# The input projection's feature blocks as seven block products instead of eight, in a hybrid mLSTM/HGRN2/attention inference step

## What is computed

```python
sh1, sc1, g1, sh2, sc2, g2 = jnp.split(ada, 6, axis=-1)
h = _rmsnorm(x, p['norm1_g']) * (1 + sc1) + sh1
proj = h @ p['w_in']
(mq, mk, mv, mo, mg, hq, hf, hi, hg, aq, ak, av, bg) = _split(proj, IN_SIZES)
```

## Time and profile before

| | |
|---|---|
| median of 3 runs | 2395.26 us (2395.05 to 2397.84) |
| the profiled execution's own time | 2394.08 us |
| its span, first to last instruction | 2392.3 us |
| mean granted PE clock | 0.993 |
| PE busy | 2318.2 us, 97% |
| DVE, ACT, POOL busy | 1274.8, 789.2, 225.4 us |

### The profile page before, as it was taken

How to read it: one execution, slowest core, us unless ns; L and a number is a source line. 1 busy time by engine, 2 the same in 40 slices (tenths; PEclk the granted TensorE clock), 3 DMA queues, 4 the chain that set the end, 5 groups by cost and what they waited for, 6 DMA issues and landing times. The chain is left out here.

```text
span 2392.3 us, 43619 instructions
## 1 busy us (share of the span) xinstructions
PE 2318.2 (97%) x17767; PEld 2142.3 (90%) x17767; DVE 1274.8 (53%) x2027; ACT 789.2 (33%) x1329; POOL 225.4 (9%) x244
## 2 busy tenths in 40 slices
PE   6999999999999899999999999998999999999997
PEld 5887779999999899889899999877999999998886
DVE  4331110102445376675455546778676676667877
ACT  5321111113333233323444445325232232234444
POOL 0000000000110011111121101000121121120001
PEclk9999999999999999999999999999999999999999
DMA  6324532215442523314100218421222122159434
GB/s 277 119 84 185 185 139 85 103 68 192 163 156 99 190 87 101 99 65 155 47 18 18 88 65 330 159 94 60 84 101 103 68 102 102 70 172 276 128 102 124
DMA packets 124748, 290.64 MB, mean 121 GB/s; under 512 B 19744, under 2 KB 63216, under 8 KB 115264
## 3 DMA queue, kind: packets, MB, share of 16 engines
q1 hardware_dynamic: 88944, 222.15, 27.3%
q10 hardware_dynamic: 31696, 51.26, 5.8%
q0 software_dynamic: 3968, 15.21, 1.7%
HBM read 205.47 MB, written 83.17 MB: 121 GB/s over the span
## 5 line engine op out<-in xcount | busy, mean ns | idle before, releaser
L62 PE MATMUL ps<-h_hi,fill_whi 128*128 128x384 f32 x672 | 234.9, 350 | 4.0 <-PEq L82 3.4
L62 PE MATMUL ps<-h_lo,fill_whi 128*128 128x384 f32 x672 | 225.8, 336 | 3.7 <-issue 3.7
L62 PE MATMUL ps<-wt 128*128 128x320 f32 (+2 forms) x1046 | 227.2, 327 | 2.3 <-DVE merged L2927 1.3
L62 PE MATMUL ps<-h_hi,fill_wlo 128*128 128x384 f32 x672 | 225.9, 336 | 0.0
L62 PE MATMUL ps<-ys,mergedr 128*128 128x256 f32 (+1 forms) x1056 | 219.2, 296 | 0.4 <-issue 0.4
L62 PE MATMUL ps<-zb,mergedr 128*128 128x320 f32 (+2 forms) x764 | 200.3, 327 | 4.9 <-issue 2.7
L62 PE MATMUL ps<-zb,wt 128*128 128x384 f32 (+3 forms) x758 | 200.2, 325 | 0.0
L62 PEld LDWEIGHTS ps<-wt 128*128 128x128 f32 x1046 | 179.6, 189 | 16.6 <-issue 2.6
L62 PEld LDWEIGHTS ps<-ys,mergedr 128*128 128x128 f32 x1056 | 174.2, 190 | 0.7 <-issue 0.7
L62 PE MATMUL ps<-prj_whi,h_hi 128*128 128x512 f32 (+1 forms) x432 | 165.4, 383 | 4.5 <-DVE h_lo L626 4.5
L62 PE MATMUL ps<-prj_wlo,h_hi 128*128 128x512 f32 (+1 forms) x432 | 162.5, 376 | 0.0
(11 more groups left out here) (459 smaller groups left out, 4800.0 us busy)
## 6 DMA issues: line engine op xcount, KB each, us to landing
wraw<-in_w_ffn_in SPq DMA_DIRECT2D x22, 1024.0 KB, 5.0
prj_raw<-in_w_ada SPq DMA_DIRECT2D x16, 1024.0 KB, 6.0
fill_raw<-in_w_fill SPq DMA_DIRECT2D x30, 512.0 KB, 4.0
wtf<-a_dram SPq DMA_DIRECT2D x55, 256.0 KB, 2.6
bg_dram<-fill_st ACTq DMA_DIRECT2D x72, 192.0 KB, 2.0
xf<-bg_dram POOLq DMA_DIRECT2D x24, 576.0 KB, 7.1
tok_dram<-prj_tst ACTq DMA_DIRECT2D x45, 256.0 KB, 2.0
prj_raw<-in_w_tok SPq DMA_DIRECT2D x10, 1024.0 KB, 6.6
```

The costliest lines, as they stand in the source:

```text
L62: mm = pe.matmul(out, lhs[a], rhs[b], start=first and n == 0, stop=last and n == 2, skip_group_check=onto)
```

## The change

The feature blocks take Strassen's scheme in Winograd's form: features in two halves, the sum's 1024 rows in two halves, tokens in two halves (576). Seven products of half-sized blocks replace eight. Four of them need sums of weight blocks (`sums`), four need sums of token blocks, called t1 to t4. The order of the products is b11, t2, b21, t3, t1, t4, b22; each runs over the tokens in two parts of 320 and 256 columns, and products 2, 5 and 6 (counted from 0) go on adding in the bank of an earlier one, once that has been copied or read.

The token sums (each 4 x 576 columns, 2304) are made by DVE, rounded by ACT and their remainders taken by DVE, most of it during blocks 4 and 5. They lie in buffers that are free then; t1 lies where a quarter of `h` was, which is stored to DRAM before and read back at the end. The weight parts of a feature block lie in seven slots in set 1 of the token blocks' weight parts. The feature stores are issued by SP instead of ACT. The diff, cut:

```diff
+        raw_t = {"t1": rows_k(both[:, 0:TS]), "t2": rows_k(g.scratch[:, 0:TS]), "t3": rows_k(wide_f[:, 0:TS]),
+                 "t4": rows_k(wide_f[:, 2 * TS:3 * TS])}
+        ORDER = ("b11", "t2", "b21", "t3", "t1", "t4", "b22")
+        Q = ((0, 320), (320, HT))
+        BANK = {0: (2, 0), 1: (3, 1), 2: (2, 0), 3: (6, 4), 4: (7, 5), 5: (6, 4), 6: (7, 5)}
+        CONTINUES = (2, 5, 6)
+        slot = [[wide[:, 8 * D + D * n + BL * s:8 * D + D * n + BL * s + BL] for s in range(2)] for n in range(7)]
...
@@ def _(sp): @@
-                if b == 5:
+                if b == 4:
+                    for n in range(2):
+                        sp.dma_start(g.part_dram[n], part(LOW, 1)[n].bitcast(F32)).then_inc(kept_out, 16)
                     sp.wait_ge(row_u, 1)
                     put(0, gf)
...
+            for f in range(NFQ):
+                if f + 2 < NFQ:
+                    weights(TB + f + 2)
+                if f == LF:
+                    sp.wait_ge(x_mm, at_mm(f, 1, 1))
+                    fill.load(sp, 2)
+                    sp.wait_ge(x_mm, at_mm(f, 4, 1))
+                    for n in range(2):
+                        sp.dma_start(part(LOW, 1)[n].bitcast(F32), g.part_dram[n]).then_inc(kept_in, 16)
+                sp.wait_ge(c22, 2 * f + 2)
+                sp.wait_ge(c21, 2 * f + 2)
+                store(f, 1)
+                sp.wait_ge(c11, 2 * f + 2)
+                sp.wait_ge(c12, 2 * f + 2)
+                store(f, 0)
             sp.wait_ge(gout, 16 * 14)
             sp.wait_ge(grow_out, 64)
-            fill.load(sp, 4)
+            fill.load(sp, 2)
+            sp.wait_ge(kept_in, 32)
...
@@ def _(pe): @@
+            for f in range(NFQ):
+                for n, name in enumerate(ORDER):
+                    pe.wait_ge(x_lo, 7 * f + n + 1)
+                    if f == 0 and name in SPLIT:
+                        pe.wait_ge(t_lo, SPLIT[name])
...
+                    for q, (lo_, hi_) in enumerate(Q):
+                        if n in READY:
+                            pe.wait_ge(READY[n], 2 * f + q + 1)
+                        elif f:
+                            pe.wait_ge(FREED[n], 2 * f + q - 1)
+                        for k in range(KH):
+                            mm = three_passes(pe, ps[:, BANK[n][q], 0:hi_ - lo_], [x[:, k * P:k * P + P] for x in slot[n]],
+                                              [x[:, lo_:hi_] for x in token_rows(name, k)],
+                                              k == 0 and n not in CONTINUES, k == KH - 1, n in CONTINUES)
+                        mm.then_inc(x_mm, 1)
...
@@ def _(act): @@
+                    if b == TB - 1 and i in (3, 6, 8):
+                        high_of({3: "t2", 6: "t3", 8: "t4"}[i])
...
+            act.wait_ge(blk_done, TB)
+            raw_ready(0)
+            for n in range(3):
+                block_hi(0, n)
+            high_of("t1")
...
@@ def _(v): @@
+            difference("t1", b12[0], b11[0], ((b12[1], ALU.add), (b11[1], ALU.subtract)))
+            v.wait_ge(gout, 16 * 14)
+            copy_rows(6)
+            difference("t2", b22[0], raw_t["t1"], ((b22[1], ALU.add),))
+            v.wait_ge(blk_done, TB - 1)
+            low_of("t2", 1)
+            copy_rows(7)
+            difference("t3", b22[0], b12[0], ((b22[1], ALU.add), (b12[1], ALU.subtract)))
...
+            rows_out(6)
+            rows_out(7)
+            low_of("t3", 2)
+            low_of("t4", 3)
...
+            v.wait_ge(blk_done, TB)
+            raw_ready(0)
+            weight_sum(0, 0)
+            block_lo(0, 0)
+            weight_sum(0, 1)
+            weight_sum(0, 2)
+            block_lo(0, 1)
+            block_lo(0, 2)
+            low_of("t1", 4)
```

More of the change, by code:

```diff
@@ L162, in front @@
         raw = [ph.sb(f"raw{i}", [P, UNIT]) for i in range(NR)]
[L163 to L168, removed]
+        with nc.sbuf_tensor("prj_wf", [P, 16 * D], F32) as wide_f:
+            pass
+        wide = ph.sb("w", [P, 16 * D], F32R)
+        w = [[wide[:, 8 * D * i + 4 * D * n:8 * D * i + 4 * D * n + 4 * D] for i in range(2)] for n in range(2)]
+        late = [wide_f[:, 8 * D + 4 * D * n:8 * D + 4 * D * n + 4 * D] for n in range(2)]
         stage = ph.sb("tst", [P, 6 * 512])
@@ L180, in front @@
         ADA = (0, 2, 1, 3)
[L181 removed]
+        ada = [x.rearrange("p (k n) -> p k n", k=KD) for x in (g.hx[:, 0:4096], g.hx[:, 4096:8192], late[0], late[1])]
         KH = KD // 2
@@ L269, in _ @@
                 sp.dma_start(m0[:], io["ml_m0"]).then_inc(gin, 16)
-            for b in range(1, NB):
+            for b in range(1, TB):
                 if b == 3:
@@ L296, in _ @@
                             sp.dma_start(g.outs["ml_m"][:, d:d + 1], ctx_m[32 * d:32 * d + HEADS, :]).then_inc(gout, 16)
+            for f in range(2):
+                weights(TB + f)
             sp.wait_ge(sum_done, 4)
@@ L582, in _, with operand @@
                         act.activation(cum, cum, ACT.Ln, bias=1.0).then_inc(lns, 1)
[L583 to L597, removed]
+            def operand(n):
+                return raw[UW[TB + n][0] % NR]
@@ L603, in _ @@
+            fill.high(act, 0)
+            fill.high(act, 1)
+            for s in range(6):
+                act.wait_ge(t_out[s], 16 * 9)
         @block.vector
@@ L727, in _ @@
             lo(3)
-            for b in range(3, NB):
-                for a in BLOCKS.get(b, ()):
+            for b in (3, 4):
+                for a in BLOCKS[b]:
                     copy_rows(a)
@@ L733, in _, with difference @@
                         columns(v, link, g, COLS, 1, col_done)
-                if b + 1 < NB:
-                    lo(b + 1)
+                lo(b + 1)
+                for a in BLOCKS[b]:
+                    if a >= 4:
+                        rows_out(a)
+            plain = lambda x: x.bitcast(F32)
+            counted = Chain(v, t_raw)
+            def difference(name, a, b, more=()):
+                to = raw_t[name]
+                counted(v.tensor_tensor(to, a, b, ALU.subtract))
+                for x, op in more:
+                    counted(v.tensor_tensor(to, to, x, op))
@@ new lines, in _ @@
+            raw_ready(0)
[6 more added lines that the diff above has]
+            low_of("t1", 4)
+            for n in range(3, 7):
+                block_lo(0, n)
+            for f in range(NFQ):
+                if f:
+                    block_lo(f, 6)
+                more = f < LF
+                if more:
+                    raw_ready(f + 1)
+                    for n in range(3):
+                        weight_sum(f + 1, n)
+                for q in range(2):
+                    first_sum(f, q)
+                    if more:
+                        block_lo(f + 1, q)
+                for q in range(2):
+                    second_sum(f, q)
+                    if more:
+                        block_lo(f + 1, 2 + q)
+                v.wait_ge(x_u2, 2 * f + 2)
+                if f:
+                    v.wait_ge(f_out[1], 16 * f)
+                result(f, 0, 4, 1, 1, u2, c22)
+                result(f, 1, 4, 1, 1, u2, c22)
+                if more:
+                    block_lo(f + 1, 4)
+                result(f, 0, 5, 1, 0, u1, c21)
+                result(f, 1, 5, 1, 0, u1, c21)
+                if more:
+                    block_lo(f + 1, 5)
```

171 lines of the change are left out of this document (148 added, 23 removed).

## The result

The changed kernel took 2398.52 us, the median of 20 runs (2393.70 to 2404.03), against 2394.12 us for the kernel before, also 20 runs (2392.20 to 2397.84): a ratio of 1.0018, 95% interval 1.0011 to 1.0025, some 4.3 us slower. Timed again with the experiments it was slower by a ratio of 1.0010 (1.0001 to 1.0019). The forecast was 2394.1 us and no measurable change. The time lies in the range given, and the difference is smaller than the 0.2% that the text called no change, but its interval excludes zero: the kernel became a little slower where it was to stay the same.

What follows compares the result with a forecast made beforehand. PE, busy 2318.2 of 2392.3 us, was taken as the bound. Terms -20.6 + 6.7 + 6.6 + 2.2 + 3.9 = -1.2 us on 2394.08 gave 2392.9, plus 1.2 to the median: 2394.1 us, range 2388 to 2401.

Steps and rivals of the forecast that it cites:

- The products: Feature stage: eight blocks at 24.97 us become eight at 22.40, the feed-forward stage's price per step; 20.6 us saved.
- The rival in which a matmul carries a smaller fixed part: Feature stage: matmuls cost N/2.4 plus a smaller fixed part; sum moves at most 2 us, to 2392.1; chance 0.04, inside "same".
- The first and the second wait: PE waits in token block 5 for DVE's row copy, 6.7 us, and before the first product for weight preparation, 6.6 us.
- Moved transfers: Row stores moved to block 4, feature stores to SP's queue, fill loads behind the last store: nothing, or 2 us at most.
- The closing restore: Stage end: two 1152 KB loads put back the tokens t1 replaced, result stores queue behind; 2.2 us, bounds 0 and 9.5.
- The rival that named the closing transfers: Stage end: restore and stores move at the crowded rate, barrier 9.5 us later instead of 2.2, total 2401.4 us; chance 0.12.
- The clock: After three idle spells of 6.5, 6.8 and 3.5 us, PE runs at half clock: 1.4 + 1.4 + 1.1, 3.9 us.
- the 1.2 us that the forecast put between the profiled run and the median: Last step of the sum: median taken 1.2 us above the profiled execution, turning 2392.9 into 2394.1 us.
- or two may follow: Clock term's caveat: each idle spell should bring one half-clock stretch, but two may follow; upper bound 3.4 us each.
- two other causes: Slower rivals: closing transfers become the bound (chance 0.12), or first-block chain or steady steps leave gaps, 2402.1 us (chance 0.05).
- The 3.7 us of the earlier trace: Kernel before: PE idle 3.7 us up to 814.5, then 3.4 us at granted clock 0.50; the clock term's source.

Runs made afterwards that it cites:

- the second group: The changed kernel once more, nothing edited, timed with the experiments against the kernel before: 2397.48 us (11 runs), ratio 1.0010.
- both edits: Changed kernel with the last row copy ahead of t2's remainder, t4 rounded earlier and first weight remainder ahead of weight sum: 2382.36 us, ratio 0.9951 against the kernel before.

## Why the prediction was wrong

**The products**: -20.6 us taken, -20.5 measured, from the price of another stage of the same kernel. The rival in which a matmul carries a smaller fixed part falls with it: a block took 22.4 us.

**The first and the second wait**: 6.7 and 6.6 us taken, 6.5 and 6.4 (7.18 less the 0.78 before) measured, link by link as added up. **Moved transfers**: nothing taken; PE shows no other idle spell of 0.3 us or more between 48 and 545 us.

**The closing restore**: 2.2 us taken, 2.8 and 3.8 in two profiles. The second load landed 4.0 us behind PE's last product of the stage, where 2.4 to 3.6 was reckoned: 10.1 us after the first was issued, against the 8.7 to 10 taken for two, whose lower end no row gave. The 576 KB stores behind them took 7.2 us, where they had taken 2.8. The rival that named the closing transfers was right in its place and not in its size: 9.5 us did not come.

**The clock** is the step that failed. The text took one stretch of 3.4 us at half clock for each wait, partly fallen into idle time, 1.4 + 1.4 + 1.1 us. The profiles show 6.8 us at each wait, which cost 5.5 us and not 3.9, and the timed runs show more than the first profile. The mean granted clock was 0.9875 over the changed kernel's 20 runs, so 2 x 0.0125 x 2397 = 60 us at half clock; in the 67 runs of the kernel before beside the experiments it was about 0.993, 33 us. Of the 27 us more, 8.5 fell on PE standing idle (3.8, 3.3 and 1.4 in the three stretches). The other 18.5 fell on work and cost some 46% of that, **8.5 us** (an estimate: the share is measured at the three waits), not 3.9. Then -20.5 + 6.5 + 6.4 + 2.8 + 8.5 = +3.7 us, against 4.3 (2.6 to 6.0) measured. The same working with the second group's clocks, 0.9878 and 0.9929, gives 7.3 us of clock and +2.5, against 2.4. The run with PE kept at work in the two waits tests the term by itself, and gives back 11.5 us (about 8 to 15 by the two intervals together) at unchanged waits.

One step on the way was a little off too: half clock was priced at half of the working time, where the rows give 46%. And the 1.2 us that the forecast put between the profiled run and the median came from three runs; over 20 runs the median is 2394.12, the profiled run's own time, so the sum really said 2392.9.

The mistake behind it was to read the price of an idle spell off one row, whose spell was 3.7 us long, and to use it for spells of 6.5 and 7.2. The words "or two may follow" were there, and the sum did not use them. The chance for slower, 0.17, came from two other causes altogether; a clock loss of two stretches a wait should have been a rival of its own. That the time still lies in the range is owed to the range's width, which those other causes had set.

**What stays open**: why the loss in the timed runs is larger than the 5.5 us that stand behind the waits in the profile. Some of it comes in stretches elsewhere: the one at 889 us is in the changed kernel's two profiles and not in those of the kernel before, of the one given a wait, or of any with a wait filled; it is there again in the four in which a wait was shortened or gone and none was filled. In each profile that has it, PE stood idle just there for 1.8 to 2.7 us, ended by nothing that the profile shows, and in none of the others for as long as 1.2 us. The first profile's row, then the second's:

```profile
889.41 0.44 PE L1564 MATMUL ps<-hgr_qp,hgr_kp 128*32 128x32 f32 x16 [2.52 <-issue]
890.88 0.33 PE L1564 MATMUL ps<-hgr_qp,hgr_kp 128*32 128x32 f32 x16 [1.84 <-issue]
```

No run tells what stops PE there. The 3.7 us of the earlier trace rows are such a spell too, and every profile taken here has at least one. Nor is it settled why the filled closing gap paid on top of both edits and not in the changed kernel.

## What to carry to other kernels

An idle spell of TensorE has two prices, its length and the work that then runs at half clock; the second was here about half of the first in sum (some 8.5 us for 15.7 us of added waiting). Where a saving is bought with waits, put the operation that TensorE waits for ahead of anything that itself waits: two reorderings here were worth 15 us. Where such a wait can't be avoided, products into an unread bank that end before it does can keep the clock; in the two first waits they did, at no cost that a run here shows. And one profile is one sample: look at the granted clock of every run before reading a difference of a few us off two profiles.

## What was not expected of the hardware

- Waits of 6.5, 7.2 and 4.1 us each had 6.8 us at half clock, which began before the wait ended. The second wait, cut to 2.6 us, had none. The length alone doesn't settle it: closing gaps of 3.31 and 3.45 us had 3.4 us and one of 3.49 had 6.8, and idle spells of 1.8 to 2.7 us at 889 us had 3.4.
- Work at half clock took 1.85 times its time and not twice: 384 columns every 320 ns, against 173.4.
- Runs of the changed kernel lay 10.3 us apart in the first comparison, those of the kernel before 5.6; in the second it was 5.0 and 7.2. Stretches of 3.4 us at half clock come and go between executions, in full work (31 and 1529 us above), here about 1 us behind an idle spell of 2.07 and 1.83 us that was there each time.
- While the restoring loads, the stores and the fill loads were in flight, the DMA engines moved some 380 to 440 GB/s for about 9.5 us, with 2 us at 220 to 250 between. The rows: 40 slices of the window from 530 to 550 us, ahead of the transfers' lines shown above:

```profile
GB/s 0 0 0 0 0 0 0 0 0 0 0 0 74 147 406 406 419 415 401 419 401 401 244 221 235 253 419 382 410 433 433 433 423 396 403 442 418 131 33 8
```
